# Hybrid encoder kernel: the first step of a differential head group, with its exponentials, its combination and its second gate half in another order

## The reference

```python
h = rms_norm(x, g)
z = h @ w_in            # q, k, v of two kinds of head groups, and a gate of width 1024
o_da = diff_attention(qd, kd, vd, lam, lam_init, subln_g)       # 4 heads of 2 x 64
o_na = neighbourhood_attention(qn, kn, vn, rpb)                 # 8 heads of 64, a 2-D window
x = x + (concat([o_da, o_na]) * silu(gate)) @ w_out
```

## Time and profile before

| what | value |
|---|---|
| median of three runs | 1508.54 us (1502.69 to 1509.71) |
| the profiled execution's own time | 1503.38 us |
| its span, first to last instruction | 1501.6 us |
| granted TensorE clock, mean | 0.990 |
| PE, DVE, ACT, POOL busy | 96%, 60%, 46%, 31% |
| w_raw loads, issue to landing, shortest, median, longest | 3.0, 3.2, 8.6 us |

### The profile page before, as it was taken

The page is one execution under the profiler, slowest core; times in us unless marked ns, Lnnn a source line. Parts: engine busy times, 40 slices in busy tenths (PEclk is TensorE's granted clock), DMA queues, the critical chain, the costliest instruction groups (busy, mean ns, idle before and its releaser), DMA issues.

```text
span 1501.6 us, 24043 instructions
## 1 busy us (share of the span) xinstructions
PE 1437.1 (96%) x8160; PEld 1170.8 (78%) x8160; DVE 895.6 (60%) x1828; ACT 684.9 (46%) x1306; POOL 459.4 (31%) x370
## 2 busy tenths in 40 slices
PE   7999999999999999899999999999999999997994
PEld 6788787878787888677887878787788888876874
DVE  6666666767655555653436667766666555557323
ACT  5445455544444444542524544544544444445330
POOL 2322223223323232313633132312322323331261
PEclk9999999999999999999999999999999999999997
DMA  4700101021111110301110001010102111121012
GB/s 175 147 29 28 43 21 49 21 60 36 45 51 55 40 59 35 133 15 57 56 47 37 24 35 35 30 40 21 53 22 74 43 52 42 52 96 58 29 56 112
DMA packets 39246, 79.41 MB, mean 53 GB/s; under 512 B 18832, under 2 KB 18832, under 8 KB 39184
## 3 DMA queue, kind: packets, MB, share of 16 engines
q1 hardware_dynamic: 39184, 78.60, 15.7%
HBM read 66.57 MB, written 15.96 MB: 55 GB/s over the span
## 4 chain that ended last, share of the span: by engine, by line
PE 87%; DVE 4%; issue 3%; ACT 2%; SPq 2%; DMA 1%; POOL 0%; DVEq 0%; POOLq 0%; ACTq 0%
PE proj L932 18%; PE proj L934 17%; PE proj L933 17%; PE scores L968 9%; PE turn L1025 5%; PE mix L1077 3%; PE mix L1078 3%; PE mix L1042 2%; PE mix L1041 2%; PE mix L1043 2%; SPq L476 2%; PE scores L1025 2%; DVE prob L1356 1%; PE mix L1051 1%; ACT prob L797 1%
## 5 line engine op out<-in xcount | busy, mean ns | idle before, releaser
L932 PE MATMUL proj<-h_hi,w_hi 128*128 128x512 f32 x1184 | 501.2, 423 | 18.3 <-DVE h_lo L1265 10.1
L934 PE MATMUL proj<-h_hi,w_lo 128*128 128x512 f32 x1184 | 467.3, 395 | 0.0
L933 PE MATMUL proj<-h_lo,w_hi 128*128 128x512 f32 x1184 | 464.3, 392 | 0.0
L932 PEld LDWEIGHTS proj<-h_hi,w_hi 128*128 128x128 f32 x1184 | 223.4, 189 | 82.9 <-issue 36.0
L934 PEld LDWEIGHTS proj<-h_hi,w_lo 128*128 128x128 f32 x1184 | 223.1, 188 | 51.6
L933 PEld LDWEIGHTS proj<-h_lo,w_hi 128*128 128x128 f32 x1184 | 224.5, 190 | 34.3
L1356 DVE CUSTOM_DVE_ANT_0 prob<-scores,inner 128x1024 f32<-128x1024 f32 (+1 forms) x192 | 204.0, 1062 | 72.1 <-PE scores L968 71.4
L577 POOL TENSOR_TENSOR w_lo<-w_raw,w_hi 128x1024 fp32r<-128x1024 f32 x78 | 191.8, 2459 | 179.5 <-ACT w_hi L730 179.4
L1364 DVE TENSOR_TENSOR pt_lo<-turn,pt_hi 128x512 fp32r<-128x512 f32 x208 | 139.2, 669 | 152.5 <-ACT pt_hi L772 151.2
L772 ACT ACTIVATE pt_hi<-turn 128x512 fp32r<-128x512 f32 x208 | 120.5, 579 | 224.4 <-PE turn L1025 223.6
L797 ACT ACTIVATE prob<-prob,nm,escale_now 128x1024 f32<-128x1024 f32 x128 | 158.0, 1235 | 3.3 <-DVE nm L1360 3.2
(11 more groups left out here) (162 smaller groups left out, 2248.8 us busy)
## 6 DMA issues: line engine op xcount, KB each, us to landing
w_raw<-chunks SPq DMA_DIRECT2D x81, 512.0 KB, 3.2
mixed_dram<-gate SPq DMA_DIRECT2D x28, 256.0 KB, 2.0
edge<-bias_dram SPq DMA_DIRECT2D x32, 224.0 KB, 3.8
h_lo<-mixed_dram SPq DMA_DIRECT2D x14, 512.0 KB, 7.5
xt<-x_t SPq DMA_DIRECT2D x8, 512.0 KB, 9.1
bias_dram<-bias_rows SPq DMA_DIRECT2D x16, 240.0 KB, 5.8
out_t<-prob SPq DMA_DIRECT2D x6, 512.0 KB, 3.0
out_t<-gate SPq DMA_DIRECT2D x2, 512.0 KB, 3.0
```

What stands on the lines that cost most here:

```text
L932: pe.matmul(dst, a_hi, b_hi, start=start, stop=False)
L933: pe.matmul(dst, a_hi, b_lo, start=False, stop=False)
L934: return pe.matmul(dst, a_lo, b_hi, start=False, stop=stop)
```

## The change

It concerns step 1 (and in part step 2) of the differential groups alone, four per layer, eight in all.
- ACT: in step 1 both exponentials of the front tile stand ahead of both `pt_hi` parts of the tile behind; before, they alternated. The tanh of the second gate half leaves the end of step 1 and stands at the end of step 2.
- DVE: `combine` of step 1 stands between the two `pt_lo` parts, ahead of the last `gated` of the group that ended; before, it followed both. `piece_part` of the second gate half leaves the end of step 1 and follows the `combine` of step 2.
- POOL: `silu` of the second gate half follows the `w_lo` of step 2.
- PE and SP keep their lists.

```diff
@@ gpsimd, attend @@
-                    if t == 1:
+                    if t == (1 if g.na else 2):
                         silu(g, 1)
@@ scalar, attend @@
+                    ahead = not g.na and t == 1
+                    if ahead:
+                        for c in range(2):
+                            exponentials(front, ft, c)
                     for c in range(2):
                         p_part(g, t - 1, c)
-                        if front:
+                        if front and not ahead:
                             exponentials(front, ft, c)
...
                         sum_squared(front, ft)
-                    if front and front.projects(ft) and ft:
+                    if not g.na and t == 2:
+                        piece_part(g, 1)
+                    if front and front.projects(ft) and ft and not ahead:
                         piece_part(front, ft)
@@ vector, step @@
                     p_part(g, t - 1, c)
+                    if c == 0 and not g.na and t == 1:
+                        combine(front, ft)
                     if c == 0 and not g.na and t % 2 == 0 and t >= 4:
                         gated(g, t // 2 - 2)
                     if c == 0 and ended and not ended.na:
                         gated(ended, PAIRS - 1)
...
-                if front:
+                if front and (g.na or t > 1):
                     combine(front, ft)
-                if front and front.projects(ft) and ft:
+                if not g.na and t == 2:
+                    piece_part(g, 1)
+                if front and front.projects(ft) and ft and (g.na or t > 1):
                     piece_part(front, ft)
```

## The result

| | runs | median | fastest to slowest | ratio to before, 95% interval |
|---|---|---|---|---|
| before | 6 | 1508.59 us | 1502.69 to 1509.71 | |
| changed | 6 | 1517.64 us | 1514.14 to 1519.47 | 1.0060 (1.0042 to 1.0079) |

The change makes the kernel 9 us slower; 1507 was predicted, with 1514 as the upper end. The profiled execution took 1514.14 us with a span of 1512.3, which is 10.7 more than before, at a mean granted clock of 0.982 (before 0.990). Of the executions reported further on, one (of e10) took 2836.2 us and is left out of its ratio.

The account below looks back on a forecast made before the run. PE was taken as the bound, its two step-2 waits as the possible win; a later load (+3.1 us), layer 1's first group (0) and layer 2's (-2.2) gave +0.9 us; 1507 was named, range 1498 to 1514.

Parts of the forecast that it names:

- What bounds, and the two waits: PE, 96% busy, loses 0.77 us to the combination and 1.45 us to `pt_lo` in step 2 of each differential group.
- Exponentials ahead: Step 1 on ACT: both exponentials end before the first `pt_hi`, cost 0; at most 2.5 us slower from layers' first groups.
- Combination and `gated`: DVE, step 1: earlier combination removes PE's first wait (-0.77 us) but moves `gated`, store and load 1.66 us later.
- The load ends last: Step 2: the load lands last, making six groups 0.22 or 0.67 us slower each, +3.1 us in all.
- The sum: Whole kernel: +3.1 + 0 - 2.2 = +0.9 us, 1504.3 on the profiled basis, 1509.4 on the median; 1507 named.
- First groups: First differential group per layer: layer 1 gains 0, second transposes staying at 73.71; layer 2 loses both waits, -2.2 us.
- The gate half in step 2 at no cost: Step 2: bank free 4.8 us after the second transposes, PE wants it at 7.6 us; tanh and `silu` also 0.
- The rival on the other side: Load landing later than 3.6 us: each microsecond costs six; at 6.2 us, 1520 on the profiled basis; chance 0.07.

Follow-up runs that it names:

- e10: Kernel before with only the second gate half moved to step 2, plus the step-2 load issued ahead of the second store: 1504.09 us, 0.9988.
- e2: Changed kernel with SP issuing the load for step 2 of a differential group ahead of the ended group's second store: 1491.49 us, 0.9904 to before.
- e1: Changed kernel with the ended group's last `gated` put back ahead of the combination on DVE in step 1: 1497.10 us, 0.9941 to before.
- e4: Changed kernel with eight additional unused 128x256 matmuls on PE ahead of the second transposes of step 2: 1508.72 us, 1.0010 to before.
- e8: Changed kernel with six of the nine matmuls that followed step 2's second transposes done ahead of them: 1509.88 us, 1.0017 to before.
- e9: e6 with the load for step 2 issued ahead of the second store: 1513.54 us, 1.0043 to before.
- e3: Kernel before with the ended group's last `gated` moved on DVE to after the combination of step 1: 1548.13 us, 1.0282.
- e6: Changed kernel with the three gate-half edits taken back, only exponentials and combination moved: 1518.09 us, 1.0070 to before.
- e5: Kernel before with only the load for step 2 issued ahead of the ended group's second store: 1507.08 us, 0.9998.

## Why the prediction was wrong

- **What bounds, and the two waits.** Right. Both were removable: e2, without the load's delay, has neither in the seven groups behind the first.
- **Exponentials ahead.** Right in the groups behind another: the first `pt_hi` starts where its transposes arrive.
- **Combination and `gated`.** Right: `gated` moved by 1.65 us (1.66 worked out), store and load with it.
- **The load ends last.** Right in mechanism; e1 and e2 show it by taking the delay away in two ways. Mis-sized a little: I took a landing of 3.2 for two groups and 3.6 for four; after the change the six take 3.5 to 3.9. (The section on the anatomy of one DMA in the Trainium skill's DMA: Bandwidth & Descriptors fits its rule to transfers that GpSimd issues; these are issued by SP. Its 3.2 us lies under all six.) In the worked group the second transposes are 0.51 us later, not 0.22 (241.75 - 1.65 - 239.59). From the first group's to the second's the distance grew by 0.49, and there is no fall between.
- **The sum.** This step failed. I wrote that the group is 0.22 us slower, as if a wait cost its length alone; the clock behind the wait was put at nothing without a reason. PE's idle time per group came as 0.60 and 1.29 us before, with nine matmuls between; now it is one piece of 2.4 to 2.9. Behind it the clock fell in five groups, 1.7 us each, 8.5 us in all. The distance between second transposes is 82.94 us before and 85.08 after one such fall: 1.71 for the clock and 0.43 for the chain. e4 and e8 take the falls away and leave the late load, and the kernel is back at 1.0010 and 1.0017. With this term my own sum would have been 1504.3 + 8.5 = 1512.8, against 1514.1 measured; that it comes so near is in part luck, as the last point shows. The term could have been had from the trace of the kernel before. In the last steps of layer 1 PE has two single waits of this size, 2.67 us and (at 631.19) 2.20 us, and the clock falls behind each. The row of the first, and the view by stretches behind it (columns as above):

```profile
621.70 0.69 PE L1088 MATMUL turn<-ident,rrec_wide 128*128 128x128 f32 x2 [2.67 <-DVE pt_lo L1364]
```

```profile
621.70:622.20 0.50, 0.50 (x2) 0.28 (x2) 0.50 (x1) 0.50 (x3) 0.00 (x0) 0.50 1.01 410
...
622.70:625.00 2.30, 2.30 (x12) 2.30 (x12) 1.56 (x2) 0.53 (x1) 0.27 (x1) 0.51 0.37 150
```

How many of the new waits would bring a fall could not be had from it: the 2.39 us of the earlier trace rows brought none.
- **First groups.** In layer 1 the second transposes start at 73.24 (predicted 73.71, as before; this load landed in 5.5 us instead of 6.2), and the first wait became a part of the second. In layer 2 both waits are gone, as predicted.
- **The gate half in step 2 at no cost.** Right as far as PE goes: no wait for its bank is listed. But I gave it no value; e9 shows that without it the late store reaches PE in another way.
- **The rival on the other side** had its price at a longer landing. It named the right place, PE's wait for the load, and the wrong price.
- **The account of the spans.** Of the 10.7 us between them, 7.9 are there at the second transposes of the last differential group (1062.13 against 1054.23). They hold four of the five falls and one more in the last steps of layer 1 (5.1 us of falls there, 3.4 before), 8.5 us in all; the late load and the first groups together come to -0.6 us, where the prediction had +0.9. The fifth fall gives 1.7 more, the rest comes in the last steps of layer 2 and the tail. The falls outside the first steps sum to 15.0 us before, 18.6 in the changed kernel, and 15.2 to 22.2 over the other profiles. Why they differ was not tried.

## What to carry to other kernels

When work moves on one engine, follow what that engine releases to the queue engine as well. Here a step moved 1.66 us later held a store, and the store held a load that had 1 us of slack; issuing the load first turns the same change from +0.6% into -1.0%. And when two short waits of TensorE merge into one long one, price the clock behind it, not only the wait; filling the wait with other work, even useless work, gave 8 us back.

## What the runs showed of the hardware

- The granted clock falls in equal portions, 1.70 to 1.71 us of full speed each, or two or three of them in a row, in all twelve profiles; only the last fall, which the end of the program cuts off, is another. Two portions (3.4 us) came where PE had stood 4.7 to 5.3 us (e3).
- The length of the idle piece alone does not tell whether it falls. It fell behind 2.59, 2.60, 2.71, 2.84 and 2.90 us in the changed kernel, and in first groups of layer 1 behind 2.20 (e6), 2.13 (e5) and 1.96 us (e9). It did not behind 2.66 and 2.38 us in the changed kernel, 2.73 in e1, 2.39 before or 2.23 in e4. The shortest single piece with a fall behind it in these steps is the 1.96 us of e9; in e8 it fell behind 1.78 and 0.80 us with 1.35 us of work between them. What decides between 2 and 3 us stays open.
- The load of 512 KB took 3.5 to 3.9 us to land in the six places where a store of 256 KB had left 0.6 to 0.9 us ahead of it. In the kernel before, with the store as close, it took 3.2 to 3.6 us there, and in e2, where it leaves long before the store, 3.1 to 3.3.
